# Late projection pieces of a hybrid decoder layer, dealt out anew over the recurrence stage, the front and the first beats

## The reference, cut to what matters

```
h   = x * (1 + sc1) + sh1
z   = h @ w_in            # queries, keys, values, gates of both branches
oa  = gated linear recurrence (8 heads, 128x128 state); its gate: silu(ga)
ob  = sparse attention: indexer -> top-k keys -> attention with queries qb
merged = sigmoid(gate_a) * oa * silu(ga) + sigmoid(gate_b) * ob
x   = LN1(ALPHA * x + g1 * (merged @ w_out))
x   = LN2(ALPHA * x + g2 * PEER(x * (1 + sc2) + sh2))
PEER: 8 heads pick 16 of 16384 experts per token; sum of g * gelu(u_e . x) * v_e
```

## Time and profile before

| | us |
|---|---|
| three runs | 2533.73, 2542.21, 2545.53 |
| their median | 2542.21 |
| the profiled execution | 2535.87 |
| its span | 2534.1 |

### The profile page before, as it was taken

The page is one execution under the profiler, slowest core; times in us unless marked ns, Lnnn a source line. Parts: engine busy times, 40 slices in busy tenths (PEclk is TensorE's granted clock), DMA queues, the critical chain, the costliest instruction groups (busy, mean ns, idle before and its releaser), DMA issues.

```text
span 2534.1 us, 26644 instructions
## 1 busy us (share of the span) xinstructions
PE 1767.0 (70%) x8475; PEld 1009.1 (40%) x8475; DVE 1466.5 (58%) x2978; ACT 625.7 (25%) x1972; POOL 634.3 (25%) x578
## 2 busy tenths in 40 slices
PE   4999989968878468744678645386425557879644
PEld 1788536556544144521335412234101113637311
DVE  1000114345564567997768999558955996353654
ACT  1010002011165343233433334222221113121221
POOL 0000000100022332222334233243424223332342
PEclk8999999668889786856768756678656676575567
DMA  9357516346497999969999998999999999999797
GB/s 318 110 199 255 174 38 203 109 172 193 151 384 262 366 361 407 383 248 376 344 423 421 383 370 328 337 418 422 389 347 389 404 389 405 401 419 390 296 422 298
DMA packets 208641, 804.93 MB, mean 318 GB/s; under 512 B 24116, under 2 KB 88468, under 8 KB 135543
## 3 DMA queue, kind: packets, MB, share of 16 engines
q0 software_dynamic: 81280, 589.48, 58.0%
q1 hardware_dynamic: 115718, 187.03, 21.3%
q10 hardware_dynamic: 11504, 26.72, 3.3%
HBM read 776.75 MB, written 28.63 MB: 318 GB/s over the span
## 4 chain that ended last, share of the span: by engine, by line
DMA 22%; PE 20%; DVE 17%; issue 10%; SPq 7%; ACT 3%; POOL 1%; ACTq 0%; DVEq 0%; another core or an unknown queue 0%; POOLq 0%
DMA uv<-in_peer_uv,eidr 12%; PE PS L1563 5%; PE PS L1516 4%; PE PS L1634 4%; DMA qbt<-mix_d 3%; SPq L1429 2%; SPq L1415 2%; DVE uv L1984 2%; SPq L1421 2%; DMA uv<-in_peer_uv,eids 2%; PE PS L1586 2%; DMA vec<-mod_d 1%; DMA wr<-in_w_oq 1%; DVE m L2014 1%; DVE st_e L662 1%
## 5 line engine op out<-in xcount | busy, mean ns | idle before, releaser
L1482 POOL DMA_INDIRECT uv<-in_peer_uv,eidr x512 | 567.8, 1109 | 1363.9 <-PE PS L1516 1064.2
L1984 DVE CUSTOM_DVE_ANT_0 uv<-uv,h2r 128x1024 f32<-128x1024 f32 x544 | 666.8, 1226 | 392.0 <-DMA uv<-in_peer_uv,eidr 313.8
L1516 PE MATMUL PS<-uv,dg 128*32 128x512 f32 x2176 | 488.9, 874 | 498.9 <-ACT dg L1798 466.4
L1516 PEld LDWEIGHTS PS<-uv,dg 128*32 128x32 f32 x2176 | 91.8, 128 | 734.0 <-ACT dg L1798 615.5
L1786 ACT ACTIVATE acts<-dots 128x2 f32<-128x2 f32 x272 | 55.2, 203 | 1062.7 <-DVE dots L1984 1043.1
L1634 PEld LDWEIGHTS PS<-h2T,wr 128*128 128x128 f32 x1280 | 201.4, 248 | 68.4 <-issue 45.8
L1634 PE MATMUL PS<-h2T,wr 128*128 128x128 f32 (+1 forms) x1280 | 213.1, 333 | 1.1 <-ACT h2T L1914 1.1
L468 PE MATMUL PS<-hT,wb 128*128 128x272 f32 (+1 forms) x608 | 143.4, 398 | 14.2 <-PEq L136 14.2
L1563 PE MATMUL PS<-htb,wr 128*128 128x416 f32 x384 | 148.4, 543 | 4.2 <-DMA wr<-in_w_late 4.2
L1798 ACT ACTIVATE dg<-fold,wts 128x32 f32<-128x32 f32 x544 | 141.1, 306 | 0.0
L468 PEld LDWEIGHTS PS<-hT,wb 128*128 128x128 f32 (+1 forms) x608 | 114.6, 190 | 45.6 <-issue 20.3
(11 more groups left out here) (374 smaller groups left out, 2155.0 us busy)
## 6 DMA issues: line engine op xcount, KB each, us to landing
wr<-in_w_oq SPq DMA_DIRECT2D x120, 512.0 KB
wb<-in_w_in SPq DMA_DIRECT2D x15, 2048.0 KB, 10.2
w_ada_p<-in_w_ada POOLq DMA_DIRECT2D x16, 1024.0 KB, 8.1
wr<-in_w_late SPq DMA_DIRECT2D x24, 512.0 KB
w_ada_b<-in_w_ada SPq DMA_DIRECT2D x8, 1024.0 KB, 21.6
h2r<-h_d ACTq DMA_DIRECT2D x32, 256.0 KB
uv<-in_peer_uv,eidr POOLq DMA_INDIRECT x512
kvr<-in_cache_kt SPq DMA_DIRECT2D x48, 128.0 KB
```

The lines of the kernel that those rows point to most:

```text
L1482: nc.gpsimd.indirect_dma_start(out=uv[j % RING][:, :], out_offset=None, in_=table, in_offset=bass.IndirectOffsetOnAxis(ids, 0)).then_inc(e ...
L1516: mm = nc.tensor.matmul(PS[row:row + ST, at:at + 512], dg[:, j % DR, :], uv[j % RING][:, D + 512 * half:D + 512 * half + 512], start=m == ...
L1984: c.step(nc.vector.tensor_tensor_reduce(out=uv[j % RING][:, 0:D], in0=uv[j % RING][:, 0:D], in1=h2r[:, q // HT % 2, g % 2, :], scale=1.0, ...
```

## The change

It numbers the late pieces anew and moves the cuts between the places.

- `D0` goes from 8 to 12: twelve pieces in the recurrence stage. Pieces 0 to 7 are now `gate_b`, 8 and 9 the first pair of `ga` and 10 and 11 the first pair of `gate_a`, which DVE multiplies there too. Pieces 8 to 11 stand between `sample_states(h)` and `sample_outputs(h)` of heads 3 to 6 (piece 7, as before, in head 2).
- `EARLY` goes from 10 to 8: the front has pieces 12 to 19, the second and third pair of `ga` and `gate_a`; seven stand between the search steps, one behind the first pick.
- The beats have twelve pieces: 20 to 23, the last gate unit, and 24 to 31, the queries. `put(0, 0.75, *lates)` puts them into beats 0 to 14, none in beats 3, 7 and 11.
- ACT applies Sigmoid or Silu in the recurrence stage where it applied Copy, and Copy to eight of the twelve pieces in the beats. `preload_act_table_set` is unchanged.

```
-D0 = 8
+D0 = 12
...
+    PAIRS = LATE // 2
+    is_raw = lambda e: 4 <= e < 12 and e % 2 == 1
+    is_silu = lambda e: 4 <= e < 12 and e % 2 == 0
+    is_query = lambda e: e >= 12
+
+    def late_chunk(d):
+        e = d // 2
+        if e < 4:
+            return 8 + d
+        if is_query(e):
+            return d - 24
+        return 16 + 8 * (e % 2) + 2 * ((e - 4) // 2) + d % 2
+
+    def late_place(e):
+        if e < 4:
+            return 1, e
+        if is_query(e):
+            return 2, e - 12
+        return 3, (e - 4) // 2
+
+    def late_function(e):
+        return (ACT.Copy, float(P) ** -0.5) if is_query(e) else (ACT.Silu if is_silu(e) else ACT.Sigmoid, 1.0)
...
-            for d in range(LRING, D0 - 2):
-                query_weights(d)
-            queries_out(0)
-            for d in range(D0 - 2, D0):
-                query_weights(d)
-            queries_out(1)
+            for d in range(LRING, 6):
+                late_weights(d)
+            pair_out(0)
+            for d in range(6, 8):
+                late_weights(d)
+            pair_out(1)
+            for d in range(8, 10):
+                late_weights(d)
             for h in range(H):
                 if h in (1, 2):
-                    queries_out(h + 1)
+                    pair_out(h + 1)
+                if h in (3, 4):
+                    late_weights(7 + h)
...
             sp.wait_ge(r_mix, 16 * 8)
+            pair_out(4)
             for i in range(3):
-                sp.wait_ge(l_sp[i], 64 if i == 0 else 32)
+                sp.wait_ge(l_sp[i], 64 if i < 2 else 32)
...
-            queries(7)
+            for d in range(7, D0):
+                pieces_out(d)
             act.wait_ge(q_o, H)
...
+            dve.wait_ge(l_ev, 4 * 6)
+            c.step(nc.vector.tensor_tensor(lstage[:, 1, :], lstage[:, 1, :], lstage[:, 2, :], ALU.mult), l_mul)
             dve.wait_ge(q_rstd, 1)
...
             for h in range(2, H):
                 sample_states(h)
-                if h == 2:
-                    queries(7)
+                if h + 5 < D0:
+                    piece(h + 5)
                 sample_outputs(h)
...
-    EARLY = 10
+    EARLY = 8
...
-    put(0, 0.8, *lates)
+    put(0, 0.75, *lates)
```

More of the change, by code:

```diff
@@ L756, in program @@
     dss_bank = lambda m: 5 + m % 2
-    l_use, l_ev = sem("l_use"), sem("l_ev")
+    l_use, l_ev, l_mul = (sem(f"l_{k}") for k in ("use", "ev", "mul"))
     l_in = [sem(f"l_in{i}") for i in range(LRING)]
@@ L849, in _, with pieces_out @@
             nc.scalar.activation(abS[:, :], abS[:, :], ACT.Exp).then_inc(q_ed, 1)
-            def queries(d):
+            def pieces_out(d):
                 e, i = d // 2, d % 2
@@ L856, in queries @@
                 main = lstage[:, e % 3, 0:6 * P].rearrange("p (t b w) -> p t b w", b=2, w=P)[:, :, i, :]
[L857 to L858 removed]
+                fn, sc = late_function(e)
+                nc.scalar.activation(main, bank(late_bank(d), 3 * P).rearrange("p (t w) -> p t w", w=P), fn, scale=sc).then_inc(l_ev, 1)
                 at = 6 * P + ST * i
[L860 to L862 removed]
+                nc.scalar.activation(lstage[:, e % 3, at:at + ST], bank(late_bank(d), ST, P, 3 * P), fn, scale=sc).then_inc(l_ev, 1)
+            pieces_out(0)
             rec.keys_out(act, 0)
[L864 removed]
+            pieces_out(1)
             rec.keys_out(act, 1)
[L866 removed]
+            pieces_out(2)
             act.wait_ge(q_kdp, 1)
             nc.scalar.activation(kdS[:, :, :], PS[0:ST, 512 * 5:512 * 7].rearrange("p (h k) -> p h k", k=P), ACT.Copy).then_inc(q_kdt, 1)
[L869 to L870 removed]
+            pieces_out(3)
+            pieces_out(4)
             for n in range(2):
                 rec.squares(act, n)
[L873 removed]
+                pieces_out(5 + n)
                 rec.inverse_root(act, n)
[L875 removed]
+            for d in range(7, D0):
+                pieces_out(d)
             act.wait_ge(q_o, H)
@@ L932, in _, with piece @@
         def _(pe):
-            def queries(d):
+            def piece(d):
                 if d == 2:
@@ L941, in queries @@
                 last.then_inc(l_use, 1)
-            queries(0)
+            piece(0)
             rec.scores(pe, 0)
-            queries(1)
+            piece(1)
             rec.scores(pe, 1)
             rec.products(pe, 0, 0, 2)
-            queries(2)
+            piece(2)
             pe.wait_ge(q_prep, 1)
@@ L956, in _ @@
             rec.products(pe, 0, 2, 4)
-            queries(3)
+            piece(3)
             rec.products(pe, 1, 0, 2)
-            queries(4)
+            piece(4)
             rec.products(pe, 1, 2, 4)
@@ L981, in _ @@
             rec.outputs(pe, 0)
-            queries(5)
+            piece(5)
             sample_states(0)
@@ L986, in _ @@
             rec.outputs(pe, 1)
-            queries(6)
+            piece(6)
             sample_states(1)
@@ L1187, in program @@
     VR = 6 * (1 + NB) + 4
-    PAIRS = LATE // 2
-    is_raw = lambda e: e >= PAIRS // 2 and e % 2 == 1
-    is_silu = lambda e: e >= PAIRS // 2 and e % 2 == 0
     E0 = D0 // 2
@@ L1193, in program @@
     nth_spill = {e: sum(1 for x in spilled if x % 3 == e % 3 and x <= e) for e in spilled}
-    nth_mul = {e: (e - PAIRS // 2) // 2 + 1 for e in range(PAIRS // 2, PAIRS)}
-    def late_chunk(d):
-        e = d // 2
-        if e < PAIRS // 2:
-            return d
-        return 16 + 8 * (e % 2) + 2 * ((e - PAIRS // 2) // 2) + d % 2
+    nth_mul = {e: (e - E0) // 2 + 1 for e in range(E0, 12)}
     landed = lambda j: 16 * (j // RING + 1)
@@ L1357, in late_spill @@
                     sp.wait_ge(b_ev, 4 * (e - E0 + 1))
-                j = 3 if is_silu(e) else 2 - e // 4
-                pair = (e - PAIRS // 2) // 2 if is_silu(e) else e % 4
+                j, pair = late_place(e)
                 at = j * P * H * N + P * H * P + pair * P * 2 * P
@@ L1841, in late @@
                 act.wait_ge(w_use, use_at[("late", 0, d)] + 1)
-                fn, sc = (ACT.Copy, float(P) ** -0.5) if e < 4 else (ACT.Silu if is_silu(e) else ACT.Sigmoid, 1.0)
+                fn, sc = late_function(e)
                 main = stage[:, e % 3, 0:6 * P].rearrange("p (t b w) -> p t b w", b=2, w=P)[:, :, i, :]
```

27 lines of the change are left out of this document (11 added, 16 removed).

## The result

| | kernel before | changed kernel |
|---|---|---|
| runs on the same chip | 4, 2533.73 to 2549.25 | 4, 2581.45 to 2594.53 |
| median | 2543.87 us | 2583.57 us |
| profiled execution, span | 2534.1 us | 2579.6 us |

A forecast was written before the change was run, and what follows sets the result against it. No engine bounds the whole, each stage has its own limit, and when the last write lands sets the time. Recurrence stage +21.3, front +1.8 and beats -16 make +7: 2546 us, range 2526 to 2566.

The forecast's parts named there:

- The beats, -16: Beats: with two pieces less, attention of tile 1 starts at about 864 instead of 880 us, -16.
- put the two equal: Beats: ScalarE's saving from 18 fewer table loads was taken as equal to its waits for a write at pieces 22 and 26.
- 26.4 us for the loads: End of the beats: tile 1's loads were to take the same 26.4 us as before and decide when attention starts.
- one of my signs of being wrong: Beats: an idle stretch gone or as long as before, where some 8 us instead of 15 was expected.
- The recurrence stage, +21.3: Recurrence stage: four more pieces and a longer end add 21.3 us, bounds +12 and +35.
- +17.4 by the middle of my bounds: Heads 3 to 6: a piece each adds +10.9 to +23.9 us, taken as +17.4.
- Rival 2: Recurrence stage: clock stays at half through heads with pieces; stage +50, total +36, 2575 us; chance 0.06.
- Rival 1: Beats: gathers delay the last write and tile 1's loads, landing only 5 us sooner; +18, 2557 us; chance 0.22.
- The front, +1.8: Front: VectorE waits for piece 19 ahead of the passes over oneh, so +1.8 us, bounds 0 and +4.
- rival 4: Front: it really loses 11 us because VectorE's wait is shorter than read; -6, 2533 us; chance 0.05.
- The table load: End of the recurrence stage: one exposed switch, 1.28 us; the skill's drain would add 1.4 to 2.8 us.
- Behind attention, 0: From attention of tile 1 to the end: moved as it is, 0; over 5 us change would count against the prediction.

The follow-up runs named there:

- e1: Changed kernel with each late pair's write issued two pieces sooner: 2557.15 us, ratio 1.0047 to the kernel before.
- e9: As e6, but GpSimd waits for tile 1's queries to land before issuing the gathers of beat 20 and later: 2525.75 us, ratio 0.9912.
- e10: Changed kernel with only a GpSimd wait for tile 1's queries before the gathers of beat 18 and later: 2569.31 us, ratio 1.0096.
- e12: As e9, but GpSimd's wait stands two beats later, at the gathers of beat 22: 2521.72 us, ratio 0.9915.
- e6: As e5, but eight pieces in the recurrence stage and sixteen in the beats, the moved multiplication being piece 15's: 2532.07 us, ratio 0.9954.
- e2: Kernel before with each late pair's write issued two pieces sooner: 2539.67 us, ratio 0.9983.
- e8: Kernel before with e2's early write, the expert weights' exponential ahead of the picks, and nine pieces in the front: 2537.75 us, ratio 0.9989.
- e11: Changed kernel with early writes, piece 19's multiplication behind the picks, and GpSimd's wait for tile 1's queries: 2536.97 us, ratio 0.9965.
- e4: Changed kernel's piece counts per stage, but the order of the kernel before (queries, gate_b, gates): 2573.78 us, ratio 1.0115.
- e3: Changed kernel with VectorE's multiplication for piece 19 moved behind the picks: 2566.43 us, ratio 1.0073.
- e7: As e5, but pieces 8 and 9 both in head 3, 10 and 11 both in head 5: 2551.66 us, ratio 1.0024.
- e5: Changed kernel with both the early writes of e1 and the moved multiplication of e3: 2544.70 us, ratio 0.9996.

## Why the prediction was wrong

**The beats, -16, measured +3.6: the step that failed.** Two assumptions carried it. The first: of the write ahead of ScalarE I said that pieces 22 and 26 keep that wait and "put the two equal". With D0 = 12 the wait comes in beat 2, where the first one in the beats had come in beat 5, while the first gathers fill the DMA engines (1.01): the write takes 16.42 us instead of 5.46, and a second one of 6.04 follows. ScalarE waited 14.16 and 7.83 us instead of 5.24 and 5.36. So the last piece ended 138.4 us behind the first values as before, where I had it 14 us sooner. e1 shows that the wait did it: without it the piece ends at 114.4 and 23.1 us come back. I had a row of the DMA engines over the beats and used it only for a bound. The second: 26.4 us for the loads, as before. They took 36.24. e9, e10 and e12 show that they are short when gathers are held back, e6 that a burst of gathers can come just when the last piece is done, and e2 and e8 that gathers issued behind the loads do little when none went out just ahead. That the beats of e1 are 156.9 us, where I had predicted some 160, is luck in part: the last piece was 10 us sooner than I had it and the loads 9 us longer. TensorE's idle stretch ahead of attention, as long as before (15.45 against 15.07), was one of my signs of being wrong.

**And what I had called the gain does not reach attention whole.** e1 against e2: two pieces less, the last one 20.5 us sooner, the beats 0.9 shorter, with the loads 26 us longer. e11 against e9, with gathers held in both: four less, the last one 19.3 us sooner (114.7 against 134.1), the beats 8.3 shorter, with TensorE waiting 15.90 and 16.55 us for rows. I had priced the end of the pieces, not the loads and the gathers that come next.

**The recurrence stage, +21.3, measured +32.4.** The heads were mis-sized: +17.4 by the middle of my bounds, measured +22.2, near the upper one (+23.9). A piece that follows the states "at once" was not in time: the clock fell in each head's states or at the piece's start, and each piece took 7.5 to 8.8 us instead of 5.83. The end was +4.1 against +4.9 (of whose parts 0.9 and 4.7 less 1.5 make 4.1 and not the 3.6 that I wrote), head 7 gave -0.5 against -1. The remaining 6.6 us need not be the change's: e8, whose instructions in this stage are those of the kernel before, comes to head 3 at 469.80, 6 us late too. In fourteen traces the clock first falls at one of three points of the same work. The traces of one piece count differ by that point:

| piece 0 of the stage took | clock falls | kernels | next stage starts |
|---|---|---|---|
| 8.54 to 8.59 us | in head 2 | before, e2, e12 (8 pieces); e4 (12) | 508.2, 510.9, 510.1; 536.6 |
| 7.82 to 8.40 us | in group 1's outputs | e6, e8, e9 (8); after, e1, e3, e10, e11, and e7 (12) | 516.6, 514.2, 516.3; 540.2 to 540.6, and 547.0 |
| 8.90 us | in group 0's outputs | e5 (12) | 547.3 |

Both orders and both piece counts are in the first two rows, so it is no matter of ScalarE's functions: e8 has Copy and the early fall, e12 has Sigmoid and the late one. In piece 0 the clock rises from half to full, so its length tells at what point of the work it rose (in the kernel before the granted clock was 0.50 from 383.00 to 386.00 and 0.97 from 386.00 to 389.30). Whether one kernel meets a row of the table more often than another does can't be told from one profiled execution of each, and stays open. With the same row, four pieces cost 24.0 us (e11 and e9, which both have the table loads at the end) or 25.7 (e4 and e2), with the longer end: some 25 is the size that the term should have had.

**Rival 2** (half clock throughout, 2575) came nearest in the number, for another reason: the clock was 0.77 in heads 3 to 6, above its own limit of 0.7. **Rival 1** had the loads held up by gathers, and its threshold of 874 was met (they landed at 919.0, or 883.5 without the 35.5 us by which the first values came later), but it did not have the write.

**The front, +1.8, measured +4.2: right in kind.** VectorE idled 12.34 us ahead of `oneh`, none but 0.44 ahead of `zs`. TensorE waited 3.79 us for piece 19's weights, and its matmuls then took 8.75 us instead of some 6. e3 shows that rival 4's 11 us were to be had (13.6), by moving one instruction.

**The table load.** The switch at the end of the stage starts at 529.21, lasts 1.28, and the activation starts at 530.50. The Trainium skill, "ScalarE: Activation LUTs", section What ACT_TABLE_LOAD costs, adds a drain of 1.38 us to each; no trace here shows one. From the mean-square matmul to the next stage it is 7.28 to 7.29 us without table loads there (before, e2, e8) and 8.58 to 8.59 with both and no pair behind (e6, e9, e12): 1.30 us for the one exposed switch, as the forecast had it.

**Behind attention, 0, measured +6.4.** I named more than 5 us as a sign against me. Over the fourteen traces this stretch took 1650.0 to 1668.3 us, with no order by edit. Part of what is gained ahead of attention may be given back there: e2 gained 18.6 us in the beats and its stretch was 9.9 longer; against e6, e9 gained 12.9 and lost 8.0, and e12 gained 14.6 and lost 18.3, though its ratio is lower (0.9915 against 0.9954). Why it varies stays open.

## What to carry to other kernels

A late write that frees a buffer should be costed at the place where it is waited for, with the transfers that fill the DMA engines just there, and not at its length elsewhere. When work that held a consumer up ends, the consumer can catch up and its producer send a burst: a load that is issued behind it pays. Holding the producer back took 14.3 us off the changed kernel (e10) and 6.3 and 7.7 off the kernels with the other edits (e9, e11); the intervals of each pair overlap, but all three go the same way. Issuing the load just ahead of the gathers may do as well (e2, e8); no run tried that alone. A piece of work put between small matmuls costs its full-clock time and more, though it raises the granted clock of the stretch.

## What the runs showed of the hardware that was not expected

The same loads for tile 1, a bias of 1 MB and queries of 512 KB, landed in 6.05 us with the gathers held (e9, e10, e11) and also with three gathers issued behind them and none in the 5.8 us ahead (e8), in 9.0 with four behind and none in the 6.5 us ahead (e2), in 12.47 with three just ahead and none behind (e12), and in 26.4 to 36.2 with gathers just ahead and behind. e4 is between: one gather 1.1 us ahead, and attention, 21.0 us behind the issue, did not have to wait. A write of 384 KB took 2.2 to 10.4 us at the end of the beats and 15.2 to 16.9 behind the first gathers.

The Trainium skill, "DMA: Bandwidth & Descriptors", section Queues, rings and completion order, says that a DMA engine takes turns between its queues packet by packet. Were a turn worth the same bytes to each, the loads would get half; my estimate from the 422 GB/s of the idle stretch is 1.5 MB at 211 GB/s, 7 us. With gathers just ahead and behind the runs show about a quarter of that rate or less (26.4 us and more), ahead of them more than it (6.05 in e8), so the turns, if it is they, are not even in bytes here.

TensorE's clock fell at 436.6 us in the changed kernel with the engine busy for 70.00 of 70.00 us, and some 14 us later, in the states of head 2, in the kernel before, with the same matmuls up to there. A piece behind 2.00 us of idle time (e7) ran at 0.77.
